# Late attention: gated tiles written to SBUF by VectorE, their high and low parts and two weight copies made by GpSimd

## The reference

```
proj = h @ w_in                     # h: normed x
y_mla  = softmax(q k^T / sqrt(96), causal) v        # 8 heads
y_diff = (softmax(.) - lam * softmax(.)) v, normed  # 4 heads, two softmaxes each
y_mem  = softmax(q m^T / 8) v                       # 4 heads, 256 memory tokens
y = concat(y_mla, y_diff, y_mem) * silu(z)
x = x + y @ w_out
```

## Time and profile before

| | |
|---|---|
| median of 3 runs | 1109.83 us (1109.31 to 1114.26) |
| the profiled execution | 1111.78 us, of which the span is 1110.0 us |
| mean granted clock of TensorE | 0.982 of full speed |
| busy, share of the span: PE | 1054.4 us, 95% |
| DVE | 627.6 us, 57% |
| ACT | 563.5 us, 51% |
| POOL | 445.8 us, 40% |
| L638 on POOL (low parts of weights) | 155 instructions, mean 2429 ns |
| L696 on ACT (high parts of weights) | 162 instructions, mean 1058 ns |

### The profile page before, as it was taken

The page is one execution under the profiler, slowest core; times in us unless marked ns, Lnnn a source line. Parts: engine busy times, 40 slices in busy tenths (PEclk is TensorE's granted clock), DMA queues, the critical chain, the costliest instruction groups (busy, mean ns, idle before and its releaser), DMA issues.

```text
span 1110.0 us, 15249 instructions
## 1 busy us (share of the span) xinstructions
PE 1054.4 (95%) x5118; PEld 874.7 (79%) x5118; DVE 627.6 (57%) x1415; ACT 563.5 (51%) x1154; POOL 445.8 (40%) x215
## 2 busy tenths in 40 slices
PE   6999889999999999999999999999999989889798
PEld 4888778899888778888888888778887778666577
DVE  4536556888835466554545455442235988586732
ACT  5443667777724344444444444443244263887821
POOL 1444552343424443444444444414444244443323
PEclk9999999999999999999999999999999999898999
DMA  5364442111013332222223223243252122343213
GB/s 198 95 175 135 132 148 76 50 47 39 30 38 133 123 104 95 95 95 94 97 94 109 95 96 133 95 141 106 98 187 103 59 88 93 100 109 86 76 49 113
DMA packets 40604, 111.87 MB, mean 101 GB/s; under 512 B 7219, under 2 KB 10419, under 8 KB 39859
## 3 DMA queue, kind: packets, MB, share of 16 engines
q1 hardware_dynamic: 29724, 91.80, 25.3%
q10 hardware_dynamic: 10824, 19.35, 5.5%
HBM read 100.25 MB, written 7.96 MB: 97 GB/s over the span
## 4 chain that ended last, share of the span: by engine, by line
issue 44%; PE 26%; POOL 15%; DVE 8%; ACT 3%; DMA 1%; SPq 1%; POOLq 1%; ACTq 0%; DVEq 0%
POOL WLO L638 13%; PE PS L1816 6%; PE PS L1818 6%; PE PS L1817 6%; PE PS L1998 2%; PE PS L2021 2%; PE PS L1957 1%; PE PS L1958 1%; DVE PB L1326 1%; DMA X<-xT 1%; PE PS L2160 1%; ACT PB L879 1%; DVE BLO L1239 1%; DVE PB L1364 1%; ACT WHI L696 1%
## 5 line engine op out<-in xcount | busy, mean ns | idle before, releaser
L638 POOL TENSOR_TENSOR WLO<-RAW,WHI 128x1024 fp32r<-128x1024 f32 x155 | 376.4, 2429 | 542.7 <-ACT WHI L696 542.5
L696 ACT ACTIVATE WHI<-RAW 128x1024 fp32r<-128x1024 f32 x162 | 171.2, 1058 | 291.6 <-PE PS L1818 260.2
L1816 PE MATMUL PS<-HHI,WHI 128*128 128x512 f32 x648 | 257.4, 397 | 12.7 <-DVE HLO L1217 9.0
L1817 PE MATMUL PS<-HLO,WHI 128*128 128x512 f32 x648 | 255.0, 394 | 0.0
L1818 PE MATMUL PS<-HHI,WLO 128*128 128x512 f32 x648 | 254.6, 393 | 0.0
L1816 PEld LDWEIGHTS PS<-HHI,WHI 128*128 128x128 f32 x648 | 123.4, 190 | 41.1 <-issue 11.5
L1816 PE MATMUL PS<-BHI,WHI 128*128 128x512 f32 x368 | 145.2, 395 | 3.2 <-POOL WLO L638 1.8
L1818 PEld LDWEIGHTS PS<-HHI,WLO 128*128 128x128 f32 x648 | 123.4, 190 | 26.3
L1818 PE MATMUL PS<-BHI,WLO 128*128 128x512 f32 x368 | 143.4, 390 | 0.0
L1817 PE MATMUL PS<-BLO,WHI 128*128 128x512 f32 x368 | 143.3, 389 | 0.0
L1817 PEld LDWEIGHTS PS<-HLO,WHI 128*128 128x128 f32 x648 | 123.3, 190 | 25.3 <-issue 0.5
(11 more groups left out here) (316 smaller groups left out, 1675.7 us busy)
## 6 DMA issues: line engine op xcount, KB each, us to landing
RAW<-wstream SPq DMA_DIRECT2D x162, 512.0 KB, 3.2
X<-xT ACTq DMA_DIRECT2D x4, 512.0 KB, 9.5
bias_b<-bias_rows ACTq DMA_DIRECT2D x2, 1024.0 KB
FX<-bias_b ACTq DMA_DIRECT2D x8, 256.0 KB, 2.8
X<-xT ACTq DMA_DIRECT2D x8, 256.0 KB, 3.7
x_keep<-X ACTq DMA_DIRECT2D x2, 1024.0 KB, 6.0
X<-x_keep ACTq DMA_DIRECT2D x2, 1024.0 KB, 5.1
outT<-X ACTq DMA_DIRECT2D x8, 256.0 KB, 2.5
```

The source lines that it names most:

```text
L638: pool.tensor_tensor(WLO[:, s, :], RAW[:, s, :], WHI[:, s, :].bitcast(F), ALU.subtract).then_inc(split_lo, 1)
L696: act.activation(WHI[:, c % 2, :], RAW[:, c % 2, :], ACT.Copy).then_inc(split_hi, 1)
L1816: pe.matmul(dst, a[0], b[0], start=first, stop=False, **kw)
L1817: pe.matmul(dst, a[0], b[1], start=False, stop=False, **kw)
```

## The change

The y of an MLA or memory map other than the last (`apart`) takes another way. VectorE writes the product with the gate into SBUF, over the gate itself (`FX[rows, ztile]`), and that releases the PSUM bank. GpSimd then makes both parts from it (`tile_parts`): a copy into `hi`, a wait on it, a subtraction into `lo`. It does so for map i-2 behind its own work for map i, and for map 18 behind everything. ScalarE's copy and VectorE's low part for these eleven maps are gone; the last map keeps the old way, with semaphores of its own. Besides, ScalarE no longer copies the first two units of `wout2`; GpSimd copies them itself and makes their low parts, in front of its work for map 2.

```diff
@@ the maps
                     m["yf"] = 1 + len([n for n in maps[:i] if "yf" in n])
+                    m["apart"] = i + 1 < len(maps)
@@ GpSimd
+            def tile_parts(m, done):
+
+                if not m.get("apart"):
+                    return
+                pool.wait_ge(wide_last, len([n for n in LATE[:done] if "latent" in n]))
+                pool.wait_ge(mem_half, len([n for n in LATE[:done] if "pair" in n]))
+                pool.wait_ge(first_held, len([n for n in LATE[:done] if n.get("mode") == "hold"]))
+                pool.wait_ge(ATT["late"]["y_f"], m["yf"])
+                rows, y = m["rows"], FX[m["rows"], m["ztile"], :]
+                pool.tensor_copy(hi(m["ytile"])[rows, :], y).then_inc(yp_hi, 1)
+                pool.wait_ge(yp_hi, m["yf"])
+                pool.tensor_tensor(lo(m["ytile"])[rows, :], y, hi(m["ytile"])[rows, :].bitcast(F), ALU.subtract).then_inc(ATT["late"]["y_lo"], 1)
+                pool.wait_ge(ATT["late"]["y_lo"], m["yf"])
+
...
-            low_halves(UNIT["down2"] + 1, UNIT["wout2"] + 2)
+            low_halves(UNIT["down2"] + 1, UNIT["wout2"])
             for m in LATE:
+                if m["i"] == 2:
+                    for c in (UNIT["wout2"], UNIT["wout2"] + 1):
+                        pool.wait_ge(raw_loaded[c % 2], 16 * (c // 2 + 1))
+                        pool.wait_ge(unit_used, c - 1)
+                        pool.tensor_copy(WHI[:, c % 2, :], RAW[:, c % 2, :]).then_inc(split_hi, 1)
+                    low_halves(UNIT["wout2"], UNIT["wout2"] + 2)
...
+                if m["i"] >= 2:
+                    tile_parts(LATE[m["i"] - 2], m["i"] + 1)
+            tile_parts(LATE[-2], len(LATE))
@@ ScalarE
-                        else:
-                            act.wait_ge(A["y_f"], m["yf"])
-                            act.activation(yt[rows, :], PS[rows, m["bank"], :], ACT.Copy).then_inc(A["y_hi"], 1)
+                        elif not m["apart"]:
+                            act.wait_ge(yd, 1)
+                            act.activation(yt[rows, :], PS[rows, m["bank"], :], ACT.Copy).then_inc(yl_hi, 1)
...
-            stream(UNIT["tail"] + 25)
-            stream(UNIT["wout2"] + 1)
             attention("late")
@@ VectorE
-                    if 0 <= i - 3 < len(maps) and "yf" in maps[i - 3]:
+                    if 0 <= i - 3 < len(maps) and "yf" in maps[i - 3] and not maps[i - 3]["apart"]:
...
-                            dve.tensor_tensor(ps, ps, FX[rows, m["ztile"], :], ALU.mult).then_inc(A["y_f"], 1)
+                            z = FX[rows, m["ztile"], :]
+                            if m["apart"]:
+                                dve.tensor_tensor(z, ps, z, ALU.mult).then_inc(A["y_f"], 1)
+                            else:
+                                dve.tensor_tensor(ps, ps, z, ALU.mult).then_inc(yd, 1)
@@ TensorE
-                            pe.wait_ge(A["y_lo"], before["yf"])
+                            pe.wait_ge(A["y_f"], before["yf"])
...
-                   2: (A["y_lo"], mla[5]["yf"]), 3: (A["y_lo"], mla[7]["yf"])})
+                   2: (A["y_lo"], mla[5]["yf"]), 3: (yl_lo, 1)})
```

More of the change, by code:

```diff
@@ L227, in build @@
         first_sums, first_held, mem_half = sem("first_sums"), sem("first_held"), sem("mem_half")
+        yp_hi, yl_hi, yl_lo, yd = sem("yp_hi"), sem("yl_hi"), sem("yl_lo"), sem("yd")
         late_hi, late_lo = sem("late_hi"), sem("late_lo")
@@ L920, in attention @@
                             if m["h"] % 2:
-                                act.wait_ge(A["y_hi"], m["y"] + 1)
+                                act.wait_ge(A["y_hi"], m["h"] + 1)
                                 act.activation(YSQ, YT, ACT.Square).then_inc(dm_sq, 1)
-                        else:
-                            act.wait_ge(A["y_f"], m["yf"])
-                            act.activation(yt[rows, :], PS[rows, m["bank"], :], ACT.Copy).then_inc(A["y_hi"], 1)
+                        elif not m["apart"]:
+                            act.wait_ge(yd, 1)
+                            act.activation(yt[rows, :], PS[rows, m["bank"], :], ACT.Copy).then_inc(yl_hi, 1)
             attention("ab")
@@ L1394, in attention @@
                                                  op0=ALU.mult, op1=ALU.mult).then_inc(dm_y, 1)
-                    if 0 <= i - 3 < len(maps) and "yf" in maps[i - 3]:
+                    if 0 <= i - 3 < len(maps) and "yf" in maps[i - 3] and not maps[i - 3]["apart"]:
                         m = maps[i - 3]
                         rows = m["rows"]
-                        dve.wait_ge(A["y_hi"], m["y"] + 1)
-                        low_from_psum(lo(m["ytile"])[rows, :], hi(m["ytile"])[rows, :], PS[rows, m["bank"], :]).then_inc(A["y_lo"], 1)
+                        dve.wait_ge(yl_hi, 1)
+                        low_from_psum(lo(m["ytile"])[rows, :], hi(m["ytile"])[rows, :], PS[rows, m["bank"], :]).then_inc(yl_lo, 1)
                     if name == "ab" and 0 <= i - 1 < len(maps):
@@ L2013, in values @@
                         else:
-                            pe.wait_ge(A["y_hi"], y - 1)
+                            pe.wait_ge(A["y_hi"], before["h"] + 1)
                 if m["first"] and name == "ab" and y > 8:
```

## The result

| | before | after |
|---|---|---|
| median | 1111.11 us (1109.31 to 1114.26, 5 runs) | 1121.69 us (1120.26 to 1122.31, 5 runs) |
| the profiled execution, span | 1111.78, 1110.0 us | 1122.31, 1120.5 us |
| ratio | | 1.0092, 95% interval 1.0076 to 1.0108 |

A forecast was written before the change was run, and what follows sets the result against it. No engine is full; hand-overs bound the late attention, in a chain of waits through VectorE and GpSimd. The terms 5.4+1.9+1.5+1.2+1.1-1.9 gave +9.2 us, on the 1109.83 median 1119.0 us; range 1110 to 1131.

The forecast's parts named there:

- The block, +5.4: Two weight copies and low halves on GpSimd delay map 2's scaling from 969.26 to 974.7: +5.4 us, up to +9.2.
- The dear copy: Rival: GpSimd's copy costs as much as a tensor_scalar, the block +9.2 us; +19.0 in all, 1128.8 us; chance 0.18.
- Map 0's and map 4's parts, +1.9 and +1.5: GpSimd's parts squeeze in among VectorE's subtractions of maps 3 and 7: +1.9 us (0 to 3.2) and +1.5 (0 to 2.8).
- The rival in which the engines don't hinder each other: GpSimd and VectorE don't slow each other and the clock holds: +3.5 us, 1113.3 us; chance 0.24.
- The four scalings of L1366, +1.2: GpSimd's parts of maps 1, 5, 11 and 15 hold up VectorE's next scalings: +1.2 us (0 to 6.4).
- the parts of the last maps: GpSimd's parts of maps 16, 17 and 18, among others, find room or work TensorE needs later: 0.
- Taken off, -1.9: Three removed instructions on the chain, VectorE's low parts at 975.58 and 992.60 and one ScalarE copy, save 1.9 us.
- The third, ScalarE's copy at 1009.62 (0.6): The removed ScalarE copy at 1009.62 on the chain of waits was counted as a gain of 0.6 us.
- the stall: VectorE waits for map 2's delayed scaling, which leaves TensorE without work for 3 us and more.
- Clock, +1.1: One more fall of TensorE's granted clock after the new idle time, half on the chain: +1.1 us (0 to 4.3).
- ScalarE's freed copies, 0: ScalarE loses two weight copies of together 2.02 us ahead of the stage's first exponentials: 0 gain.
- The rival of the other side: Shorter VectorE steps regain 7.6 us everywhere and TensorE keeps full clock twice: -6.5 us, 1103.3 us; chance 0.12.

The follow-up runs named there:

- e2: The kernel before with only the weight block moved to GpSimd in front of map 2, tiles the old way: 1116.14 us, ratio 1.0052.
- e4: The changed kernel with GpSimd's parts of maps 0 and 4 put off behind its work for maps 5 and 9: 1117.79 us, ratio 1.0066.
- e7: e5 without ScalarE's left-over wait on the value matmuls for split maps, and map 11's parts behind map 15's turn: 1110.74 us, ratio 0.9998.
- e5: The changed kernel with the weight block before map 0 and the parts of maps 0 and 4 made later: 1113.66 us, ratio 1.0031.
- e3: The changed kernel with the weight block before map 0 in place of map 2: 1116.55 us, ratio 1.005.
- c2: The changed kernel run again without an edit, for a second profile: 1123.58 us, ratio 1.0108.

## Why the prediction was right, and where it was not

The sum for the stage was +9.2; two executions show +7.5 and +9.9. The measured time lies 2.7 us above the forecast. Of that 1.3 us is the base: the sum was set on a median of 1109.83 us over three runs, which over five came out at 1111.11. Against that the change costs 10.6 us (10.2 by the ratio), and it includes a loss ahead of the stage, 3.0 us in the profiled execution, that no row of the kernel before could show. Step by step:

- **The block, +5.4: right in kind and place, a little too dear.** Map 2's scaling starts 23.31 us into the stage in place of 18.62: +4.69, and e2 has +4.71 at map 4. The copy takes 1.03 us where I had taken 1.23 from the select; the two copies, the two low halves and the scaling follow each other without the 0.2 I allowed for waits (970.30 to 976.99, 6.69 us in place of 7.3). The dear copy fell with it. The Trainium skill (GPSIMD Engine Reference, "Engine selection") calls one-input work there roughly line-rate; the trace agrees: ScalarE's own copy of this tile takes 1.06 us. It holds for the copy alone: a scaling with a factor for each partition, which has one tile as input too, takes 1.57 us for half the columns.
- **Map 0's and map 4's parts, +1.9 and +1.5: shown.** The subtractions grew from 1.94 to 3.38 and 3.20, by 1.44 and 1.26, a quarter and a sixth less than priced. e4 takes both away. The rival in which the engines don't hinder each other falls. The Trainium skill (SBUF — State Buffer, "Who interferes with whom") calls the shared port pair an exclusive lock; the rows agree in VectorE's subtractions and in e4's four-column product, and what reads PSUM kept its 0.69; the scaling at 987.34, below, isn't held for the 0.24 us that such a lock would ask.
- **The four scalings of L1366, +1.2: too dear.** Three took 0.91 in place of 0.88 twice and 1.20 in place of 0.88, the fourth (map 18's, at 1060.78) 0.76 in place of 0.61: +0.5 in all. e7 gets 0.33 back for the third. The sum put what the parts of the last maps cost at nothing, and there it missed something: GpSimd's two scalings of map 18 now meet VectorE's scaling of map 19 and take 2.15 us in place of 1.83. The transposes that wait for them start 3.33 us behind map 18's reciprocal in place of 2.79, 0.4 us more than the fourth scaling explains. For map 1 GpSimd's second part (L670 at 986.30, 1.28 us) is not through when VectorE's scaling starts at 987.34, 0.24 us ahead of its end, and still the scaling takes only 0.03 more: an overlap by the clock isn't a price by itself.
- **Taken off, -1.9: half wrong, and this is the step that failed.** The two low parts (0.6 and 0.7) are in the numbers: map 4 is late by less than lock and block together, and in e5 the stage gains them. The third, ScalarE's copy at 1009.62 (0.6), brought no gain but a loss of 0.92 us, and a second one of 0.64 at the same place behind map 17. I had read the copy as a duration on the chain and taken it off. What stood behind it was a table load, which until then ran for the most part beside VectorE's reciprocal (0.61 us of it showed), and the wait that stayed pushed the load wholly behind the reciprocal. Term by term: -0.6 became +0.92 + 0.64 = +1.56, 2.2 us of miss. I hadn't asked what is late next once the copy is gone, as I had for the stall.
- **Clock, +1.1: a size between bounds that the case doesn't fix.** The fall that I named came at 30 us, in all five profiles with the stall (and a shorter one in e3, without it). Then later ones went elsewhere: 3.4 us more at half clock in after, 10.2 more in c2, 3.4 less in e2. From map 4 to 6 the steps show +0.49 in after and +1.80 in c2; later 0.5 (after, map 9 to 10) and 2.9 (e2) are given back. As a term of a sum this should have been a range of -3 to +3.
- **ScalarE's freed copies, 0: right.** Map 0 comes 1.86 us early, map 3 no earlier (+0.19, -0.06).

The errors within the stage ran against each other: block, parts and scalings 2.1 us too dear (0.7 each), the table load 2.2 us and the late scaling of GpSimd 0.4 us missed. The 2.4 us between +7.5 and +9.9 arise in one kernel, for the most part where the clock fell differently. That the sum is near is in part luck. The rival of the other side, that shorter steps count everywhere, is refuted with its own condition: e5 and e7 show what the removal of eleven low parts is worth without the new obstacles, 2.05 us up to map 11 and 2.72 in all, not 7.6.

**What stays open**: why edits of the late code, even one without work, lose time in the first 320 us of the program (1.3 to 5.5 us in the ten profiles). It makes e7, whose stage is the shortest of all, no faster as a whole; whether a version of it with the old start would be at about 1108 wasn't tried.

## What to carry to other kernels

Where work is moved to a slower engine, its position in that engine's queue is worth more than its length: 6.7 us of it cost 4.7 in front of a step that others wait for and 0.2 to 0.8 two maps earlier. Before you count a removed instruction as a gain, look at what stands behind it and at each wait it leaves over: a wait that nothing needs can keep a table load from being done in idle time. And before a change of less than 0.5% is judged, time the old kernel with an edit that does nothing.

## What the runs showed of the hardware

- As built here, with two waits ahead of the square root, one of them stands ahead of ScalarE's table load of 1.28 us, which then can't be done in idle time: square root 1.38 us behind its input, against 0.03 with one wait.
- A VectorE product of 128x4 with both inputs in SBUF took 1.23 us beside a GpSimd subtraction that ended 0.02 us before it, and 0.16 us without one.
- The granted clock fell in stretches of 3.4, 6.8 or 10.2 us, and all but the first of them lay elsewhere in one kernel than in another: the sum at 1.2 GHz in the twelve profiles listed was 17.0 to 34.0 us, and differed by 6.8 between two executions of the same kernel.
- Twelve waits already fulfilled, in late code of GpSimd, made the program 0.24% longer (0.11 to 0.38), with the loss ahead of them in time.
